# Up stages of block 1: x as the stationary operand, 512 weight columns streaming, the result transposed back

## The reference

```python
D_MODEL, SEQ, DEPTH, D_FF = 1024, 256, 2, 2816

def swiglu(x, w_up, w_down):
    a, b = jnp.split(x @ w_up, 2, axis=-1)
    return (jax.nn.silu(a) * b) @ w_down

for i in range(DEPTH):
    x = layer_norm(ALPHA * x + 0.5 * swiglu(x, ffn1_up[i], ffn1_down[i]), ln1_g[i], ln1_b[i])
    mix = token_mix(x, ...)
    x = layer_norm(ALPHA * x + mix, ln2_g[i], ln2_b[i])
    ple = jax.nn.sigmoid(x @ w_ple_gate[i]) * (p[i] @ w_ple[i])
    x = layer_norm(ALPHA * x + 0.5 * swiglu(x, ffn2_up[i], ffn2_down[i]) + ple, ln3_g[i], ln3_b[i])
```

## Time and profile before

| | |
|---|---|
| Median of 3 runs | 2595.23 us (2593.11 to 2595.92) |
| Profiled execution | span 2594.2 us from its first to its last instruction, 39608 instructions |
| PE busy | 2569.4 us (99%), 16037 matmuls, as many weight loads |
| DVE, ACT, POOL busy | 1340.3 (52%), 784.0 (30%), 78.6 (3%) |
| HBM read | 696.47 MB, 271 GB/s over the span |

### The profile page before, as it was taken

How to read it: one execution, slowest core, us unless ns; L and a number is a source line. 1 busy time by engine, 2 the same in 40 slices (tenths; PEclk the granted TensorE clock), 3 DMA queues, 4 the chain that set the end, 5 groups by cost and what they waited for, 6 DMA issues and landing times.

```text
span 2594.2 us, 39608 instructions
## 1 busy us (share of the span) xinstructions
PE 2569.4 (99%) x16037; PEld 1903.5 (73%) x16037; DVE 1340.3 (52%) x1735; ACT 784.0 (30%) x1319; POOL 78.6 (3%) x103
## 2 busy tenths in 40 slices
PE   9999999999999999999999999999999999999998
PEld 9989898999999999999999988833333333333333
DVE  6866785687788668657854684312112112112112
ACT  4414441443344144423423363122121121121111
POOL 0000200000000020000001000100000000000000
PEclk9999999999999999999999999999999999999999
DMA  7685344456655843345563636799999999999998
GB/s 231 211 285 179 139 153 146 146 178 224 230 192 182 314 154 130 130 149 176 180 207 119 231 123 245 300 376 426 427 427 428 427 428 427 427 428 427 427 427 368
DMA packets 264396, 702.27 MB, mean 271 GB/s; under 512 B 13012, under 2 KB 155296, under 8 KB 215008
## 3 DMA queue, kind: packets, MB, share of 16 engines
q1 hardware_dynamic: 249616, 650.03, 65.0%
q0 software_dynamic: 12496, 46.90, 5.0%
q10 hardware_dynamic: 2176, 3.83, 0.5%
HBM read 696.47 MB, written 6.60 MB: 271 GB/s over the span
## 4 chain that ended last, share of the span: by engine, by line
PE 83%; DMA 9%; SPq 5%; DVE 1%; issue 1%; ACT 1%; DVEq 0%; ACTq 0%
PE acc L1954 11%; PE acc L1149 6%; PE mix L1153 6%; PE acc L1151 6%; PE acc L1969 5%; PE acc L1222 5%; PE acc L1238 4%; SPq L978 4%; PE mix L1143 3%; PE acc L1121 3%; PE acc L1095 3%; PE acc L1172 2%; PE acc L1689 2%; DMA ring<-in_w 2%; PE acc L1180 2%; PE acc L1178 2%
## 5 line engine op out<-in xcount | busy, mean ns | idle before, releaser
L1149 PE MATMUL acc<-branch_parts,area_parts 128*128 128x256 f32 x1176 | 344.3, 293 | 0.2
L1153 PE MATMUL mix<-big_parts,zz_parts 128*128 128x256 f32 x1176 | 332.9, 283 | 0.0
L1151 PE MATMUL acc<-area_parts,ring_parts 128*128 128x256 f32 x1176 | 332.6, 283 | 0.0
L2642 DVE TENSOR_TENSOR ring_parts<-ring,area_parts 128x1792 fp32r<-128x1792 f32 (+2 forms) x139 | 262.8, 1890 | 98.7 <-ACT area_parts L2139 60.9
L3504 DVE COPY zz<-acc 128x512 f32<-128x512 f32 x32 | 22.1, 692 | 525.7 <-PE acc L1954 525.7
L1149 PEld LDWEIGHTS acc<-branch_parts,area_parts 128*128 128x128 f32 x1176 | 225.1, 191 | 9.3 <-DVE big_parts L2642 0.8
L1151 PEld LDWEIGHTS acc<-area_parts,ring_parts 128*128 128x128 f32 x1176 | 225.3, 192 | 0.2
L1153 PEld LDWEIGHTS mix<-big_parts,zz_parts 128*128 128x128 f32 x1176 | 225.1, 191 | 0.0
L2139 ACT ACTIVATE area_parts<-ring 128x1792 fp32r<-128x1792 f32 (+1 forms) x116 | 189.6, 1634 | 16.6 <-DMA ring<-in_ffn_up 12.3
L2735 DVE SCALAR_TENSOR_TENSOR zz_parts<-area_parts,ring_parts 128x1792 fp32r<-128x1792 f32 x84 | 170.2, 2026 | 6.3
L2131 ACT ACTIVATE area<-acc 128x512 f32<-128x512 f32 (+1 forms) x67 | 32.1, 479 | 342.0 <-PE acc L1883 331.9
(11 more groups left out here) (595 smaller groups left out, 4931.4 us busy)
## 6 DMA issues: line engine op xcount, KB each, us to landing
ring<-in_ffn_up SPq DMA_DIRECT2D x86, 1024.0 KB, 5.0
big<-in_w SPq DMA_DIRECT2D x77, 1024.0 KB, 25.7
ring<-in_w SPq DMA_DIRECT2D x76, 1024.0 KB, 25.7
ring<-in_w_in SPq DMA_DIRECT2D x72, 1024.0 KB, 7.0
area<-in_w SPq DMA_DIRECT2D x58, 1024.0 KB, 25.7
spare<-in_w SPq DMA_DIRECT2D x38, 1024.0 KB, 25.5
area<-in_w_ada POOLq DMA_DIRECT2D x24, 1024.0 KB, 7.6
ring<-in_ffn_down SPq DMA_DIRECT2D x28, 768.0 KB, 5.0
```

Source lines behind the costliest of these rows:

```text
L1149: pe.matmul(abank(a, b)[:, ts], wg[:, b, k, c * P:c * P + P], xg[:, k, :], start=c == 0 and k == 0, stop=False, skip_group_check=True)
L1151: pe.matmul(abank(a, b)[:, ts], wl[:, k, c0:c0 + P], xl[:, k, :], start=False, stop=k == K - 1, skip_group_check=True)
L1153: mm = pe.matmul(kbank(a, b)[:, ts], wk[:, b, k, c * P:c * P + P], xk[:, k, :], start=False, stop=k == K - 1, skip_group_check=True)
L2642: return v.tensor_tensor(out, a, b, op)
```

## The change

Within the up stages x becomes the stationary operand and the 512 columns of a unit stream past it. A result then has 128 tokens on the partitions and 512 hidden columns along (`a` in columns 0 to 255, `b` in 256 to 511), and the two banks of a group hold the two halves of the tokens. PE transposes the finished product of silu(a) and b back (four 128 x 128 transposes a unit) and ACT copies it to `big`. The weights are split in three pieces along the contraction (chunks 0 to 2, 3 and 4, 5 and 6), each with 512 columns, where they were two halves by columns. The transfers of a unit are cut the same way, chunks 0 to 2 and 3 to 7. Unit 0 of ffn1 is turned too (`first_product`). The gate and projection stages keep the weights as the stationary operand.

```diff
+PIECES = ((0, 3), (3, 5), (5, SPLIT))
@@ transfers
             def up_half(L, w, r, c, hf):
+                v = view(L, r).rearrange("p (k two c) -> p k two c", two=2, c=256)
+                k0, k1 = ((0, PIECES[0][1]), (PIECES[0][1], DC))[hf]
+                for two in range(2):
+                    c0 = two * D_FF + c * 256
+                    sp.dma_start(v[:, k0:k1, two, :], w[:, L * DC + k0:L * DC + k1, c0:c0 + 256]) \
+                        .then_inc((landed, landed_2)[hf][turn_of(L, r) % 2], 16)
...
+                    if n == 2 and s == 0:
+                        banks(L, b0 + 2)
+                    else:
+                        sp.wait_ge(piece_used, pieces_used(L, s, n - 2, 0))
+                    up_half(L, up_w, r0 + n, n, 0)
+                    banks(L, b0 + 2 * (n - 2) + 2)
+                    up_half(L, up_w, r0 + n, n, 1)
@@ PE
+            def first_product(L, between):
...
+                        mm = pe.matmul(abank(a, h), x[:, k, half(h)], w[:, k, :], start=k == 0, stop=k == DC - 1)
+            def turn(L, s, n, i=0):
+                a = split_group(s, n)
+                pe.wait_ge(rows_ready, 11 * (2 * L + s) + (n + 1) + i * 2)
+                for c in range(2):
+                    for b in range(2):
+                        c0 = c * T + b * P
+                        mm = pe.transpose(abank(a, 1)[:, c0:c0 + P], rows[:, b, c * P:c * P + P], ident)
+                mm.then_inc(turned, 1)
+            def up_product(L, s, u, i=0):
...
+                half_landed(pe, L, r, 1, i)
+                for b in range(2):
+                    for k in range(SPLIT, DC):
+                        pe.matmul(kbank(a, b), x[:, k, half(b)], w[:, k, :], start=k == SPLIT, stop=False, skip_group_check=True)
+                for p, (k0, k1) in enumerate(PIECES):
+                    pe.wait_ge(k_ready, piece_parts(L, s, u, p) + i * 6)
+                    for b in range(2):
+                        for k in range(k0, k1):
+                            pe.matmul(abank(a, b), xg[:, k, half(b)], wg[:, k, :], start=k == 0, stop=False, skip_group_check=True)
+                            pe.matmul(abank(a, b), xl[:, k, half(b)], wl[:, k, :], start=False, stop=k == SPLIT - 1,
+                                      skip_group_check=True)
+                            mm = pe.matmul(kbank(a, b), xk[:, k, half(b)], wk[:, k, :], start=False, stop=k == SPLIT - 1,
+                                           skip_group_check=True)
+                        if p == 2:
+                            mm.then_inc(acc_done, 1)
+                    if p < 2:
+                        mm.then_inc(piece_used, 1)
+                    if p == 1 and u > 0:
+                        turn(L, s, u - 1, i)
@@ PE, down stage (the same in down_part of the first one)
                         if at == 5:
                             mm.then_inc(half_used, 1)
+                            if u == 0:
+                                turn(L, s, 10)
@@ ACT, silus
                 for n in range(1 - s, 11):
                     a = a0 + n
                     if n < 10:
+                        for p in range(2):
+                            act.wait_ge(piece_used, pieces_used(L, s, n, p))
+                            upper_piece(L, s, n + 1, p)
+                    if n:
+                        copy_turned(L, s, n - 1)
+                    bank_done(act, L, a, 1)
+                    if S * 11 + n:
+                        act.wait_ge(rows_ready, S * 11 + n)
+                    copy(joined, both_banks(mix, a)).then_inc(k_summed, 1)
+                    if n < 10:
+                        upper_piece(L, s, n + 1, 2)
                     act.wait_ge(a_joined, 38 * L + (27 + n + 1 if s else n))
+                    act.activation(joined[:, :, 0:256], joined[:, :, 0:256], ACT.Silu).then_inc(silu_ready, 1)
...
+                copy_turned(L, s, 10)
@@ DVE, hidden
                 for n in range(1 - s, 11):
+                    if n < 10:
+                        for p in range(2):
+                            lower_piece(L, s, n + 1, p)
+                    join_unit(L, s, n)
+                    if n < 10:
+                        lower_piece(L, s, n + 1, 2)
+                    hidden_rows(L, s, n, joined[:, :, 256:512])
```

More of the change, by code:

```diff
@@ L641, in turn_of, with unit_transfers, transfers @@
             return r - sum(u < r for u in APART) if L < LAYERS else r
+        def unit_transfers(L, r):
+            up = r < UP1 + 11 or UP2 <= r < UP2 + 11
+            return 2 if L < LAYERS and up and (L, r) != (0, UP1) else 1
+        def transfers(L, r):
+            ringed = [(l, q) for l in range(LAYERS) for q in range(UNITS) if q not in APART] + [(LAYERS, q) for q in range(12)]
+            upto = ringed.index((L, r)) + 1
+            return sum(unit_transfers(*unit) for unit in ringed[:upto] if turn_of(*unit) % 2 == turn_of(L, r) % 2)
         def half_landed(eng, L, r, hf, i=0):
@@ L1104, in product_halves @@
                 group_open(pe, L, a)
-                pieces = L == 0 and r == UP1
-                if not pieces:
-                    unit_landed(pe, L, r)
+                unit_landed(pe, L, r)
                 w = view(L, r).rearrange("p (k c) -> p k c", c=UC)
@@ L1126, in product_halves @@
                             between()
-            def split_product(L, s, u, i=0):
+            def first_product(L, between):
+                r, a = UP1, G_UP1
+                group_open(pe, L, a)
+                if L:
+                    unit_landed(pe, L, r)
+                w = view(L, r).rearrange("p (k c) -> p k c", c=UC)
+                for h in range(2):
+                    for k in range(DC):
+                        if L:
+                            pe.wait_ge(x_ready, L * 48 + (8 * h + k + 1))
+                        elif not h and k % 2 == 0:
+                            pe.wait_ge(x_piece[k // 2], 16)
+                            if k < 6:
+                                pe.wait_ge(first_piece[k // 2], 32)
+                            else:
+                                unit_landed(pe, L, r)
+                        mm = pe.matmul(abank(a, h), x[:, k, half(h)], w[:, k, :], start=k == 0, stop=k == DC - 1)
+                        if between is not None and h == 0 and k == 1:
+                            between()
+                    mm.then_inc(acc_done, 1)
@@ L1268, in ffn @@
                         down_part(a, part, [abank(a, c)[:, 0:T] for c in range(2)], lambda kk: big[:, kk, :],
-                                  last=(lambda c, mm: mm.then_inc(acc_done, 1)) if part else None)
+                                  last=(lambda c, mm: mm.then_inc(acc_done, 1)) if part else None,
+                                  between=(lambda: turn(L, 0, 10)) if g == 0 and not part else None)
                     if n == 2 and g == 1 and L == LAYERS - 1:
@@ L2735, in lower, with lower_piece @@
                 v.scalar_tensor_tensor(out=wk[:, hf], in0=g, scalar=-1.0 / STEP, in1=l.bitcast(F32), op0=ALU.mult, op1=ALU.add) \
+                    .then_inc(k_ready, 1)
+            def lower_piece(L, s, n, p):
+                ks = slice(*PIECES[p])
+                l, g = unit_piece(L, s, n, p, ring_parts), wg[:, ks].bitcast(F32)
+                v.wait_ge(g_ready, piece_parts(L, s, n, p) - (1 if s == 0 and (n, p) == (1, 0) else 0))
+                tt(l, unit_piece(L, s, n, p, ring), g, ALU.subtract)
+                v.drain()
+                v.scalar_tensor_tensor(out=wk[:, ks], in0=g, scalar=-1.0 / STEP, in1=l.bitcast(F32), op0=ALU.mult, op1=ALU.add) \
                     .then_inc(k_ready, 1)
```

181 lines of the change are left out of this document (92 added, 89 removed).

## The result

The changed kernel takes 2611.78 us, the median of 4 runs (2609.15 to 2613.07). The kernel before takes 2594.39 us in its 4 runs (2593.11 to 2595.92). The ratio is 1.0065, 95% interval 1.0053 to 1.0077: 0.65% slower, where 2581.3 us was forecast and 2600 was the upper end of the range. The profiled execution was the quickest of the four; its span is 2607.4 us, against 2594.2 of before. The 4.2 us by which the medians differ more can't be seen in one profile.

What follows compares the result with a forecast made beforehand. Up stages were taken as pure PE issue, each microsecond counting at the end. Terms -42.3 - 0.3 - 1.2 + 19.2 + 10.7 = -13.9 took the span to 2580.3 us, median 2581.3; range 2570 to 2600, near 0.88.

Steps and rivals of the forecast that it cites:

- (a): Up stages: 42 split matmuls of 512 columns at 0.216 us replace 84 of 256 at 0.120 per unit; -42.3 us.
- (g): Ends of up stages: PE waits 3.6 us for the first split down weights in three of four down stages; +10.7 us.
- rival: 5: Down stages: the clock halves after each new wait, 1.8 us each, 5 in all, giving 2586.7 us; chance 0.10.
- a rival with 0.06: Up stages: the 13 ns per split instruction stay, 0.227 us each; +18.5 on the forecast, 2599.8 us; chance 0.06.
- The rival of 0.240 a matmul: Up stages: a 512-column split matmul takes 0.240 us, so widening wins nothing; +28.4, 2623.6 us; chance 0.07.
- (b): Eighth row chunk in plain fp32, -0.3 us in all; the two first products with wider instructions, -1.2 us for both.
- (c): Up stages and first products: four added transposes in each of 44 units, 0.109 us each; +19.2 us.
- The rival of 0.272 apart: Transposes in the units start one duration apart, 0.272 us; 28.7 us more than forecast, 2610.0 us; chance 0.03.
- (d): DVE and ACT within an up unit: DVE 10.7 us of PE's 11.2, slacks of 1.4 to 3.4 us; cost 0.
- (e): Weight transfers of up units: larger second part issued later, slack 2 us, and one more issue at the start; cost 0.
- DVE becomes the bound: Up-stage loop: a unit of 11.5 us gives 2593 us, one of 11.8 gives 2606; chance 0.10.
- (f): First unit of each stage: in the second layer the x sum ends earlier as PE wants it earlier; cost 0, within 0.5.

Runs made afterwards that it cites:

- The series: Two kernels: the changed kernel with series of matmuls, varied in kind and width, added ahead of layer 0's first down stage; the first took 2696.16 us.
- the tenth series: Split matmuls over acc, acc and mix behind fp32 matmuls, added to the changed kernel before layer 0's first down stage; nine spacings 0.230 us, thirty 0.2267.

## Why the prediction was wrong

The frame held: no wait of PE in the up stages behind their first product, every microsecond on PE came out at the end, and the largest new wait was named and sized. Term by term, on the spans (forecast -13.9, measured +13.2, a miss of 27.1):

| step | forecast | measured | miss |
|---|---|---|---|
| (a) split matmuls of 512 columns | 9.07 us a unit, -42.3 | 11.78 - 1.72 - 0.44 = 9.63 a unit | +23.5 |
| (g) waits | +10.7 | 10.6 | -0.1 |
| clock behind the waits | 0 (rival: 5) | 6.4 | +6.4 |
| fall of the clock at 1676 | as before (no term) | gone; 1676.14 to 1686.37 was 10.23 us, now 1690.56 to 1699.66, 9.10 | -1.1 |
| wait of 1.1 us for DVE at 937, between layer 1's up stages | as before (no term) | gone; one of 0.4 is new between layer 0's | -0.7 |

These add up to 28.0; 0.9 us is left open.

(a) is the step that failed. It said that "a load hides wholly under 213 ns of streaming and not quite under 107", and so took 0.216 from the fp32 instruction that streams equally long. The series show that this is not what sets the spacing of these matmuls: the split kind has 13.4 ns on top at 512 columns and 13 at 256, the fp32 kind 2.5 at either of its widths, and loads of 135 or 108 ns in place of 188 bring nothing. The 5 ns that the prediction read off fp32 matmuls of 128 columns (0.112) may be another thing: transposes (0.109) and split matmuls of 128 columns (0.111) are spaced about the same, with half the streaming. What the 13 ns are, no run shows. The nearest row was not that of equal streaming but that of the same kind: 0.120 less 256/2.4 = 13 ns, kept, gives 0.227. The prediction had this as a rival with 0.06 (its +18.5 is the same sum as the 18.9 below). Of the 23.5 us, 42 x 42 x 0.0107 = 18.9 are the rate, and 42 x 0.11 = 4.6 the slower matmuls behind changes of kind, which no step had. The measured average in a unit, 9.63/42 = 0.229, lies above the prediction's own break-even of 0.224. The rival of 0.240 a matmul falls too: that would be no gain at all, and 0.44 us a unit is one.

The Trainium skill ("TensorE: Matmul & The Clock Gate", section "Part 2: What happens when you issue a matmul") gives N/2.4 + 2.5 ns between matmuls back to back at the full clock. That is 215.8 for 512 columns, which the fp32 instructions of equal streaming show to the digit (215.8) and the split ones don't (226.7). Here the measurement decides.

(b) Two first products: layer 1's lasts 718.74 - 704.14 = 14.60 us to the next unit, before 714.99 - 699.83 = 15.16. Layer 0's goes from 20.99 - 5.57 = 15.42 to 20.69 - 5.65 = 15.04, with 0.4 us more of waiting for its weights in it. That is about the 0.6 of each. (c) was right: 0.45 a unit by leaving them out. The rival of 0.272 apart falls: a duration isn't a spacing. (d) was right: no wait of PE for a piece or for the rows, DVE idle 1.6 us a unit. So was (e), but for those 0.4 us. (The terms of DVE's sum come to 10.9 us with all its gaps, not 10.7; measured it is 10.2.) The same unit length as before (11.8) was also what the rival "DVE becomes the bound" would give; the idle DVE and the fp32r spacing tell them apart. (f) was right within its 0.5. (g) was right in its place, its cause and its size. It was priced as idle time alone, though, and the clock was put in a rival of 0.10 at 1.8 us each; it measured 2.1 on average, and came with all three waits. With that rival and the one of 0.227 together, 5 + 18.5 on the forecast, the prediction would have said 2605.

Where the shift arises is seen in the starts of the stages, before and after: first down stage 139.46 to 138.52 (-0.9), second 625.10 to 623.72 (-1.4), layer 1's first product 699.83 to 704.14 (+4.3), its first down stage 833.19 to 836.58 (+3.4), the product behind that stage 907.87 to 918.31 (+10.4), the fourth down stage 1316.02 to 1324.29 (+8.3), what follows it 1385.12 to 1399.02 (+13.9). Up stages win 0.8 to 1.2 us each, part of it because the last unit's transposes now lie in the down stage; the three down stages that split lose 5.6 to 7.1, as 3.5 of wait, 1.6 to 3.1 of clock and 0.44 of transposes give.

## What to carry to other kernels

Take the fixed cost of an instruction from a row of the same kind of operand, not from one that streams as long; it is the row's spacing less its columns over the clock. Where a change moves an in-order engine's instruction behind something that arrives later, price the wait and the clock behind it, and look first whether the instruction queued behind can go ahead: here one call moved in ACT's order was worth 18 us. And before a layout is turned for the sake of wider matmuls, set 13 ns per saved instruction against 109 ns per transpose: with 42 saved and 4 added it is 0.56 against 0.44 us, which the 0.11 behind the changes of kind uses up.

## What was not expected of the hardware

- Split (fp32r) matmuls start 13 to 14 ns more than their columns apart, from 256 to 512 columns, whatever the bank, and at 256 in either orientation; fp32 instructions 2.5 ns.
- Fewer stationary columns don't help: 230 and 232 ns with 64 and 32, 226.7 with 128, though the record of a load shrinks from 188 to 135 and 108 ns.
- 128 streamed columns of the split kind are some 111 ns apart, hardly less than 256 (120).
- Behind fp32 matmuls or transposes, some ten split matmuls of 512 columns come at 0.232 instead of 0.227 us in the kernel; the tenth series shows it behind fp32 matmuls with all other engines quiet. With 256 columns this doesn't show.
- Each of three waits of 3.5 us went with a stretch of PE at 1.2 GHz, which began within the wait or up to 0.6 us behind it; with the same stretch filled by matmuls the clock stayed at 2.4 GHz.
